# Forgetting attention's scores: from one float32 product to rounded high and low parts, with a ring of three head pairs

## The reference, cut to what matters

```python
def _fox_branch(x, w_in, b_f, w_out):
    q, k, v = ...                         # x @ w_in, (B, S, 16, 64) each
    log_f = jax.nn.log_sigmoid(f_logit + b_f)
    cum = jnp.cumsum(log_f, axis=1)
    o = _dense_causal(q, k, v, FOX_HEAD_DIM ** -0.5, cum).reshape(B, S, W)
    return (o * jax.nn.silu(gate)) @ w_out
...
        s = jnp.einsum('bqhd,bkhd->bhqk', q_blk, k, preferred_element_type=jnp.float32) * scale
        s = s + c_q[..., :, None] - cum_t[:, :, None, :]
        s = jnp.where(k_pos[None, :] <= q_pos[:, None], s, NEG_INF_2)
        p = jax.nn.softmax(s, axis=-1)
```

## Time and profile before

| what | value |
|---|---|
| median of 3 runs | 1881.92 us (1878.97 to 1882.63) |
| the profiled execution, its own time | 1878.35 us |
| its span | 1876.5 us |
| PE busy | 1817.3 us, 97% |
| PEld busy | 1451.9 us, 77% |
| DVE busy | 938.9 us, 50% |
| ACT busy | 747.3 us, 40% |
| POOL busy | 622.1 us, 33% |
| mean granted clock | 0.992 |

### The profile page before, as it was taken

One profiled execution on the slowest core, in us unless ns is written; L12 is line 12 of the kernel. 1 busy time (PEld: TensorE's weight loads), 2 busy tenths in 40 slices (PEclk: granted clock), 3 DMA queues, 4 the chain that ended last, 5 costly groups with the idle time before them and its releaser, 6 DMA issues.

```text
span 1876.5 us, 24992 instructions
## 1 busy us (share of the span) xinstructions
PE 1817.3 (97%) x10060; PEld 1451.9 (77%) x10060; DVE 938.9 (50%) x1976; ACT 747.3 (40%) x1617; POOL 622.1 (33%) x296
## 2 busy tenths in 40 slices
PE   7998999999999999999999999989999999999997
PEld 5787876778888888889766888868777777886666
DVE  5556766553311101144767366755634243576664
ACT  4333355454331222334445344453243233345452
POOL 4332421144444443443212333324332324322122
PEclk9998999999999999999999999999999999999999
DMA  6222321043333332323212232213322222321211
GB/s 182 82 74 57 95 53 29 29 133 115 113 101 101 90 113 83 97 85 96 52 40 72 79 93 68 68 46 90 101 68 59 79 67 85 93 58 44 52 57 67
DMA packets 215171, 148.45 MB, mean 79 GB/s; under 512 B 51968, under 2 KB 197392, under 8 KB 215056
## 3 DMA queue, kind: packets, MB, share of 16 engines
q1 hardware_dynamic: 210160, 135.27, 25.8%
q10 hardware_dynamic: 4896, 11.60, 1.7%
HBM read 144.74 MB, written 2.10 MB: 78 GB/s over the span
## 4 chain that ended last, share of the span: by engine, by line
PE 82%; DVE 12%; ACT 4%; DMA 1%; issue 1%; POOL 0%; ACTq 0%; DVEq 0%; SPq 0%
PE PS L392 21%; PE PS L394 21%; PE PS L393 21%; PE PS L538 7%; PE PS L484 5%; PE PS L568 4%; DVE X L1446 1%; ACT sq L1025 1%; PE PS L542 1%; DVE sm L1908 1%; PE PS L701 1%; DVE XTl L1454 1%; DVE X L1460 1%; DVE P L1922 1%; ACT P L1357 1%
## 5 line engine op out<-in xcount | busy, mean ns | idle before, releaser
L2005 POOL TENSOR_TENSOR Wl<-Wr,Wh 128x1024 fp32r<-128x1024 f32 (+5 forms) x292 | 621.9, 2142 | 1220.3 <-ACT Wh L972 1219.9
L392 PE MATMUL PS<-XTl,Wh 128*128 128x512 f32 (+1 forms) x1096 | 413.6, 377 | 10.8 <-DVE XTl L1454 9.3
L394 PE MATMUL PS<-XTh,Wh 128*128 128x512 f32 (+1 forms) x1096 | 409.0, 373 | 0.0
L393 PE MATMUL PS<-XTh,Wl 128*128 128x512 f32 (+1 forms) x1096 | 408.7, 373 | 0.0
L972 ACT CAST Wh<-Wr 128x1024 fp32r<-128x1024 f32 (+5 forms) x292 | 267.5, 936 | 177.3 <-PE PS L394 138.6
L392 PEld LDWEIGHTS PS<-XTl,Wh 128*128 128x128 f32 x1096 | 207.2, 189 | 54.8 <-issue 12.7
L394 PEld LDWEIGHTS PS<-XTh,Wh 128*128 128x128 f32 x1096 | 207.1, 189 | 36.6
L393 PEld LDWEIGHTS PS<-XTh,Wl 128*128 128x128 f32 x1096 | 207.3, 189 | 34.5
L392 PE MATMUL PS<-Wl,XTh 128*128 128x512 f32 (+2 forms) x608 | 229.4, 377 | 3.7 <-DVE XTl L1454 1.8
L394 PE MATMUL PS<-Wh,XTh 128*128 128x512 f32 (+2 forms) x608 | 225.7, 371 | 0.0
L393 PE MATMUL PS<-Wh,XTl 128*128 128x512 f32 (+2 forms) x608 | 225.6, 371 | 0.0
(11 more groups left out here) (317 smaller groups left out, 2478.8 us busy)
## 6 DMA issues: line engine op xcount, KB each, us to landing
Wr<-in_w_in SPq DMA_DIRECT2D x38, 512.0 KB, 3.8
Wr<-in_fox_w_in SPq DMA_DIRECT2D x32, 512.0 KB, 4.1
Wr<-in_w_ffn_gate SPq DMA_DIRECT2D x22, 512.0 KB, 4.0
Wr<-in_w_ffn_up SPq DMA_DIRECT2D x22, 512.0 KB, 3.8
Wr<-in_w_ffn_down SPq DMA_DIRECT2D x22, 512.0 KB, 3.6
Wr<-in_swa_w_in SPq DMA_DIRECT2D x20, 512.0 KB, 3.9
Wr<-in_mla_w_in SPq DMA_DIRECT2D x16, 512.0 KB, 4.0
Wr<-in_mla_w_out SPq DMA_DIRECT2D x16, 512.0 KB, 3.5
```

The source lines that it names most:

```text
L392: pe.matmul(o, l[0], r[1], start=start, stop=False)
L393: pe.matmul(o, l[1], r[0], start=False, stop=False)
L394: return pe.matmul(o, l[0], r[0], start=False, stop=stop)
L2005: raw.tensor_tensor(l[:, 0:m], r[:, 0:m], h[:, 0:m].bitcast(F), sub).then_inc(*weight_lo.next(i))
```

## The change

Queries and keys of a pair are kept as fp32r tiles, in three sets that are used in turn (pair x uses set x % 3). For head u, `f_Q[..][u]` has the rounded queries of that head on both halves of the partitions, `f_K[..][u]` has the rounded keys on the head's own half and what the rounding left of them on the other half, and `f_QL` has what the rounding left of the queries, each head on its own half. The float32 product is replaced by two: queries high (twice) against keys high and low on 128 rows, and queries low against keys high on 64 rows. Filling the tiles takes four ScalarE instructions for a pair where there was one, two copies and two subtractions on VectorE where there was one copy, and two more VectorE instructions (`rests`) for the low part of the queries. From pair 3 on both engines wait for the scores that last used the set. The bank of the queries' projection is now released by VectorE.

```diff
-            f_QT, f_KT = alloc(cm, "QT", [128, 8, T]), alloc(cm, "KT", [128, 8, T])
+
+            f_Q, f_K = ([[alloc(cm, n, [128, T], R) for _ in range(2)] for _ in range(3)] for n in ("QT", "KT"))
+            f_QL = [alloc(cm, "QL", [128, T], R) for _ in range(3)]
...
-                            ((s, "q0"), w[:, :, 0:128], [(by_act, (s, "q0"))]), ((s, "k0"), w[:, :, 1024:1152], [(by_dve, (s, "k0"))])])
+                            ((s, "q0"), w[:, :, 0:128], [(by_dve, (s, "q0"))]), ((s, "k0"), w[:, :, 1024:1152], [(by_dve, (s, "k0"))])])
...
-                    proj_T((s, x), w[:, :, tile(f)], XT, x_ready, (by_act, (s, x)))
+                    proj_T((s, x), w[:, :, tile(f)], XT, x_ready, (by_dve, (s, x)))
...
-                    scores(s, x, [(lambda u, i, n: (f_QT[half(u), x, tile(i)], f_KT[half(u), x, 0:n]), alternate),
+                    scores(s, x, [(lambda u, i, n: (f_Q[x % 3][u][:, tile(i)], f_K[x % 3][u][:, 0:n]), alternate),
+                                  (lambda u, i, n: (f_QL[x % 3][half(u), tile(i)], f_K[x % 3][u][half(u), 0:n]), alternate),
                                   (lambda u, i, n: (CB[0][:, tile(i)], MB[u][:, 0:n]), alternate)],
-                           [by_act.at(s, f"q{x}"), by_dve.at(s, f"k{x}"), by_dve.at(s, "mb", x, 1)])
+                           [by_dve.at(s, f"q{x}"), by_dve.at(s, f"k{x}"), by_dve.at(s, "mb", x, 1)])
...
-                act.mul((s_QT if s == "swa" else f_QT)[:, f, :], bank[s, x][:, :], 0.125).then_inc(*by_act.next(s, x))
+                if s == "swa":
+                    act.mul(s_QT[:, f, :], bank[s, x][:, :], 0.125).then_inc(*by_act.next(s, x))
+                else:
+                    if f >= 3:
+                        after(scores_full, s, f - 3, 1, 3)
+                    for h in range(2):
+                        for u in range(2):
+                            act.mul(f_Q[f % 3][u][half(u ^ h), :], bank[s, x][half(u), :], 0.125).then_inc(*by_act.next(s, x))
...
-                    copy(f_KT[:, f, :], bank[s, x][:, :], s, x)
+                    if f >= 3:
+                        e.wait_ge(scores_full.at(s, f - 3, 1, 3))
+                    for u in range(2):
+                        copy(f_K[f % 3][u][half(u), :], bank[s, x][half(u), :])
+                    e.wait_ge(by_dve.now())
+                    for u in range(2):
+                        low(f_K[f % 3][u][half(1 - u), :], bank[s, x][half(u), :], f_K[f % 3][u][half(u), :], s, x)
+
+            def rests(x, f):
+
+                e.wait_ge(by_act.at("fox", x))
+                for u in range(2):
+                    ve.scalar_tensor_tensor(f_QL[f % 3][half(u), :], bank["fox", x][half(u), :], 0.125,
+                                            f_Q[f % 3][u][half(u), :].bitcast(F), mult, sub).then_inc(*by_dve.next("fox", x))
...
+            rests("q0", 0)
             keys(s, "k0", 0)
...
+                elif x[0] == "q":
+                    rests(x, f)
```

## The result

The changed kernel takes 1884.53 us (median of 11 runs, 1881.60 to 1889.65) against 1878.97 us before; the ratio is 1.0031 (95% interval 1.0020 to 1.0043), which is 5.8 us slower (3.8 to 8.1). A second measurement beside the experiments gave 1.0030 (1.0018 to 1.0043). The forecast was +3.3 us and a time of 1885.2 us, range 1880.5 to 1889.5. The profiled execution is one of the long ones, 1888.92 us.

What follows compares the result with a forecast made beforehand. TensorE, busy 97% of the span, was taken to bound the kernel. Products -1.3, score 0 +0.8, score 1 +2.1 and clock +1.7 summed to +3.3 us, 1885.2 us from the median; range 1880.5 to 1889.5.

Steps and rivals of the forecast that it cites:

- The products: Score matmuls of each pair: 2.40 us against 2.56, a gain of 0.16 us a pair, -1.3 us for eight.
- the change to half rows: TensorE going from full to half rows: 0.12 us, twice per pair before and after, so it cancels.
- Half-row heads side by side: New half-row product: two heads assumed to run in pairs like float32, 0.58 us second group, 0.45 first.
- single file: Rival: half-row fp32r products of the two heads do not overlap, +4.8 us on the forecast, 1890.0; chance 0.10.
- loads in the open: Rival: full-row loads not hidden, four more of 0.11 us a pair in the second group, +3.5 us; chance 0.02.
- four passes: Rival: the rounded product runs in four passes, 3.2 us a pair, +25 us; chance 0.01.
- Score 0: Ahead of pair 0's scores: six VectorE filling instructions delay the value copies and `MB`, +0.8 us.
- the slip in the decay chain: Rival: ScalarE's new instructions move GpSimd subtractions beside VectorE casts, some +2 us; chance 0.12, shared with a second half-clock stretch.
- Score 1: Ahead of pair 1's scores: the whole filling of `keys` is in the open, +2.1 us, stall 3.0 us.
- Pairs 2 to 7: Later pairs: nothing added, since a gate projection and a turn cover the filling of keys.
- The clock: TensorE after the stalls: one stretch of 3.4 us at 1.2 GHz likelier than none, +1.7 us.
- rival of a second stretch: Rival: another half-clock stretch, score 0 too, some +2 us on the forecast, 1887; chance 0.12, shared with a decay-chain slip.

Runs made afterwards that it cites:

- the products alone: The two new products, with tiles filled as before (one ScalarE, one VectorE instruction a pair, low parts left out); ratio 0.9990 against the kernel before.
- the second profile: Another profiled execution of the unmodified changed kernel, the fastest of seven executions; span 1879.4 us.
- the filling alone: The changed kernel's new tiles filled in full, but one float32 product of the high parts as scores; ratio 1.0031 against the kernel before.

## Why the prediction was right, and where its size was off

- **The products.** Right in sign and size: -1.6 us for -1.3. Measured are 0.64, 0.98, 0.43 and 0.61 us for 0.48, 0.89, 0.45 and 0.58. The full-row ones came out longer, because the distances there include the change to half rows, 0.12 us, that the forecast had cancelled against the one before; with it they are 0.60 and 1.01. So by the distances alone the new products are 0.10 us longer than the old one (2.66 against 2.56), and the gain is what stands ahead of them: the mask ahead of the second group fell from 0.32 to 0.20 us, and the turn ahead of the first from 2.28 (1412.97 to 1415.25) to 2.10.
- **Half-row heads side by side.** Assumed without a row; right, by the starts 0.003 us apart and the 0.61 us. The rivals of single file, of loads in the open and of four passes fall with the products alone.
- **Score 0.** The step was right, the size short: MB was to be 0.8 us later; the stall grew by 1.8, and by 1.1 in the second profile. 0.3 us is spacing (0.72 and not 0.67). The other 0.7 us of the first profile is not the slip in the decay chain that the forecast had among its rivals: from VectorE's first use of the gate bias `FB` to the first of the six instructions it is 21.2 us in the first profile and 21.3 in the second, and before the change it was 21.3 to the copy of k0. The whole chain began later, because its first instruction waited longer for the transfer of `FB`. These are the rows of the two profiles, first and second:

```profile
DVE FZ L1962 <- DMA FB<-in_fox_b_f: 5.3, 1, 5.3
DVE FZ L1962 <- DMA FB<-in_fox_b_f: 4.4, 1, 4.4
```

With the old filling such a late start cost nothing: the wait is 4.4 us before and 5.4 with the products alone, and the stall is 1.5 us in both. The gaps between the value copies, which the new filling uses up, had absorbed it.

- **Score 1.** +2.1 us forecast, 3.04 for 0.88 measured: right.
- **Pairs 2 to 7.** No new wait: right, and the run with g0 moved shows the price without the cover that was named, 0.9 us at once at score 2.
- **The clock.** This is the term that was mis-sized. The forecast took one stretch of 3.4 us, 1.7 us; it had seen that the stalls would put it at risk but took the shorter kind of stretch, and one only. Measured, the clock's part is some 4 us: stretches of 6.8 us occur, and after both stalls. The trace of the kernel before had held one already, around an idle time of 5.0 us:

```profile
1227.11 2.08 PE L895 MATMUL PS<-KT,QT 64*128 64x256 f32 x8 [4.99 <-DVE GT L1531]
1224.00:1230.80 6.80, 3.69 (x24) 2.87 (x26) 4.98 (x16) 2.50 (x5) 2.35 (x1) 0.50 0.23 78
```

The earlier trace rows shows only the shorter one. The rival of a second stretch had 0.12 and was nearer the truth than the forecast. In the second profile the forecast's single stretch of 3.4 us is what came.

- **The verdict.** Because of that term the forecast stood at +3.3 us, just inside the 0.2% that it took as no change; the result, +0.31% (0.20 to 0.43), is just outside. The chances of 0.58 and 0.37 leaned the wrong way.
- **The time itself was luck.** 1885.2 us is 0.7 us from the measured 1884.53, but it was counted from a median of 3 runs, 1881.92, which is 3 us above the 1878.97 of 11 runs measured beside the change. From the latter the forecast is 1882.3, still in the range and 2.3 us short. The base that was too high and the sum that was too small, by its clock term above all, cancelled.

## What to carry to other kernels

When heads already share the array side by side, count the passes per pair of heads before replacing float32: four passes two abreast against one full and one half was a gain of 0.2 us in 2.6, and the gain can be smaller than what filling the operands costs in one place without cover. Look at the first items of a pipelined list, not at its steady state; moving one call ahead of four copies removed a stall of 3 us here. Where TensorE is to stand still for some 3 us, reckon with up to 2 us more a time for the clock, look for the longest stretch of low clock in the trace at hand and not for the mildest, and price it from the granted clock of many runs.

## What the runs showed of the hardware

Idle times of equal length are not followed by equal clocks. The stall of 3.0 us ahead of score 1 was followed by 6.8 us at 1.2 GHz in one profile and 3.4 us in another of the same kernel; the same stall by none in the profile of the filling alone, one of 2.7 us by none, and one of 1.5 us, in the profile of the products alone, by a stretch of 3.4 us. Before each the engine had been idle for the times named; what else decides was not tried. With matmuls in the idle time whose result is dropped, the granted clock stayed at 1.00 from 1345 to 1400 us and 4.1 us of 1880 came back; the scores started 0.16 us after `MB` was done, as they do without them (0.14).

VectorE's instructions of 64 x 512 out of one PSUM bank stand 0.72 us apart, whether they round, copy or subtract, and its copies of 128 x 512 out of four banks 0.60 us (four in 2.48).
